# Memory attention's softmax placed ahead of its value tiles, and the first value tile of the recurrence placed ahead of its diagonal products

## The chip, the cores and the metric

The kernel runs on one core of one Trainium2 chip. The metric is the device time of one execution in microseconds (us), as the median of several runs. The profile is one further execution, recorded by the hardware profiler.

## What is computed

The reference is a stack of transformer layers over 256 tokens of width 1024, all in float32: a gated feed-forward layer, a mixer of two attentions, cross attention over 256 memory tokens, a second feed-forward layer, then an RWKV-7 layer (the recurrence), a squared-ReLU layer, sliding-window attention and a last squared-ReLU layer. The change touches the cross attention and the recurrence:

```python
def memory_cross_attention(h, mem_n, w_q, w_kv, w_o):
    b, s, _ = h.shape
    q = (h @ w_q).reshape(b, s, MEM_HEADS, MEM_HEAD_DIM) * (MEM_HEAD_DIM ** -0.5)
    k, v = jnp.split(mem_n @ w_kv, 2, axis=-1)
    k = k.reshape(b, -1, MEM_HEADS, MEM_HEAD_DIM)
    v = v.reshape(b, -1, MEM_HEADS, MEM_HEAD_DIM)
    p = jax.nn.softmax(jnp.einsum('bshd,bmhd->bhsm', q, k).astype(jnp.float32), axis=-1)
    o = jnp.einsum('bhsm,bmhd->bshd', p.astype(v.dtype), v).reshape(b, s, D_MODEL)
    return o @ w_o
```

There are 4 memory heads of width 256. In the recurrence, `r, k, v` are three products with token-shifted inputs, the keys are scaled and normalised per head (`kk / max(sqrt(sum(kk * kk)), 1e-12)`), `g` is a two-step low-rank gate, and per head the state is updated token by token:

```python
    def step(S, inp):
        r_t, w_t, k_t, v_t, a_t, b_t = inp
        sa = jnp.einsum('bhvk,bhk->bhv', S, a_t)
        S = S * w_t[:, :, None, :] + sa[..., None] * b_t[:, :, None, :] + v_t[..., None] * k_t[:, :, None, :]
        y = jnp.einsum('bhvk,bhk->bhv', S, r_t)
        return S, y
```

The kernel computes it by chunks of 128 tokens: 16 heads times 2 chunks give 32 triangular matrices that are inverted, from 32x32 blocks on the diagonal outwards.

## The kernel before

**Weights.** All weights stream through a ring of four slots, one tile of 128x2048 floats (1 MB) each. A large product is done in three passes (`product`, L355 to L357): the weights are split into a high part (copy on ScalarE, L305, `heads_after`) and a low part (subtraction on VectorE, L315, `rests_after`), half a tile at a time, into four half slots. `heads_after(done)` and `rests_after(done)` issue every split whose slot was freed by a half tile of index below `done`; since engines run their instructions in order, a call that waits for TensorE to end a tile stops everything behind it on that engine. `multiplied(g)` waits for tile g's products (`tile_done`, which counts two per tile). The value tiles of the recurrence and the tile `lora_g` are used whole (`arrived_raw`), without a split; each of their products takes all of float32's passes.

**Memory stage** (`memory_stage`, L1745). TensorE: four key tiles, four query tiles, the scores of two token halves t (L1814) in banks 0 to 3, four value tiles in banks 4 to 7 (`col_to_natural`), with the transposes of the weights of half 0 (`turn(0)`, L1788) after the third value tile and of half 1 after the fourth, then the value products (L1828), t by t, head by head, once every value tile is copied, then the output tiles (`out_stage("memo")`), which wait for the split of the values: three of four parts ahead of the first tile. VectorE: `largest(t)` scales the scores and takes the maximum (L1877, L1880), `weigh(t)` divides by the sum (L1884, L1886). ScalarE: exponentials with sums (L1851), copies of the value tiles (L1857), of the turned weights (L1862) and of the values (L1867). On ScalarE the exponentials of half t stand in round n = 8 + t, behind `heads_before` of that round, which waits for the first value tile in round 8. Softmax and value tiles are interleaved in the same rounds.

**Recurrence, projections** (`rwkv_projections`, L1991). After the last key tile, TensorE sums the squares of the keys (L2230), does the tail of the gate's first product (L2217), waits for the inverse norms, spreads them over the channels (L2238) and does the rest of the gate's first product (`lora_g_in`, L2223). ScalarE takes the root of the sums (L2350) and two sigmoids (L2352, L2353). VectorE makes `undirected` (L2147), `decayed` (L2150) and one column (L2172), then the inverse norms (L2175 and the reciprocal L2176), two parts of keys and reads, and multiplies by the spread norms (L2181, L2182). The stage is a block of its own: all engines meet at its end.

**Recurrence, inverses** (`rwkv_inverses`, L2379). TensorE: diagonal 32x32 products (L2453) and 128x128 grams (L2444) in two rounds, two more grams, the gate's second product (L2465, L2469), then the value tiles as fillers: `values()` is a generator that issues one of its 64 products (L2481) per step, and `fill(n)` issues n of them between the groups of small products; `fill(16)` ahead of the bonus (L2493) and the transposes `turn(0)`, `turn(1)`, further ones after the step products (L2524), the 32-row products (L2534), the narrow (L2542, L2544) and cross products (L2553 to L2555), and four in each round of the last loop (L2563, L2568). VectorE solves the diagonal blocks in a long chain (`solve_blocks`, L2730) and turns the result by L2632 (`t16`), for which L2524 waits. Its small copies follow each group. POOL clears buffers.

Engines synchronise by semaphores (`wait_ge`, `then_inc`); `at(k)` counts from the stage's start, `since(k)` from a mark.

Of the kernel before, what the change touches and what calls it, by code (L numbers as in the profile page):

```python
# [25 lines left out]
P = 128  # L26
SEQ = 256
TT = SEQ // P
D = 1024
KC = D // P  # L30
# [8 lines left out]
MEM_HEADS = 4  # L39
# [1081 lines left out]
def mixer_section(e):  # L1121
    nc = e.nc
    with ExitStack() as stack:
# [40 lines left out]
        out_stage(e, "memo", om, [("ffn2_norm", e.hT)], ready=e.sig("memory_split"), needs=(3, 3, 4, 4))  # L1164
# [579 lines left out]

def memory_stage(e, memory, om):  # L1745
# [18 lines left out]
    with Open(nc) as block, ExitStack() as stack:  # L1764
# [9 lines left out]
        def _(pe):  # L1774
# [42 lines left out]
            for n in range(4):  # L1817
                col_to_natural(e, pe, g_v + n, memory.T, 4 + n)
                if n == 2:
                    turn(0)  # L1820
            turn(1)
            for t in range(TT):
                pe.wait_ge(*turned_copied.at(t + 1))
                pe.wait_ge(*evacuated[0].at(8))
                for h in range(MEM_HEADS):
                    for c in range(2):
                        for kb in range(TT):
                            mm = pe.matmul(e.ps[:, 2 * t + h // 2, span(2 * (h % 2) + c, P)],  # L1828
                                           memory.vm[:, kb, span(2 * h + c, P)], pT[t][:, h, kb, :],
                                           start=(kb == 0), stop=(kb == TT - 1))  # L1830
                    if h % 2:
                        mm.then_inc(*values_ready.one())

        @block.scalar
        def _(act):
# [4 lines left out]
            for n in range(12):  # L1840
                heads_before(e, act, g_k + n + 1)
# [5 lines left out]
                if n in (8, 9):  # L1847
                    t = n - 8
                    act.wait_ge(*max_ready.at(t + 1))
                    for h in range(MEM_HEADS):  # L1850
                        x = act.activation(scores[t][:, h, :], scores[t][:, h, :], ACT.Exp, bias=stat[:, t, 0, h:h + 1],  # L1851
                                           accum_out=stat[:, t, 1, h:h + 1])
                    x.then_inc(*sums_ready.one())
                if n >= 8:
                    multiplied(e, act, g_k + n)
                    for t in range(TT):
# [3 lines left out]
            for t in range(TT):  # L1860
                act.wait_ge(*turned.at(t + 1))
                act.activation(pT[t].rearrange("p h k n -> p (h k n)"),  # L1862
                               e.ps[:, 2 * t:2 * t + 2, :].rearrange("p b n -> p (b n)"), ACT.Copy).then_inc(*turned_copied.one())
            heads_after(e, act, 2 * (g_k + 12))
            for b in range(4):
                act.wait_ge(*values_ready.at(b + 1))
# [4 lines left out]
        def _(dve):  # L1871
# [22 lines left out]
            for n in range(12):  # L1894
                if n == 8:
                    largest(0)
                rests_before(e, dve, g_k + n + 1)
# [17 lines left out]
            for b in range(4):  # L1915
                dve.wait_ge(*headed.at(b + 1))
                at = (ALL, span(b % 2, 4), span(b // 2, P))
                dve.tensor_tensor(om[1][at], e.ps[:, b, :].rearrange("p (c n) -> p c n", c=4), om[0][at].bitcast(F32),
                                  ALU.subtract).then_inc(*split.one())
# [70 lines left out]

def rwkv_projections(e, w):  # L1991
# [13 lines left out]
    gained, before_ready = e.sig("hidden_ready"), e.sig("hidden_hi_ready")  # L2005
# [28 lines left out]
    with nc.Block() as block:  # L2034
# [13 lines left out]
        def _(dve):  # L2048
# [115 lines left out]
            undirected(2)  # L2164
            multiplied(e, dve, first[K] + 3)
# [8 lines left out]
            dve.wait_ge(*root.at(2))  # L2174
            link.done(dve.tensor_scalar(inv[:, 0, :], inv[:, 0, :], 1e-12, None, ALU.max))  # L2175
# [1422 lines left out]
```

## Time and profile before

| | us |
|---|---|
| median of 3 runs | 1420.87 (1419.27 to 1429.3) |
| time of the profiled execution | 1425.83 |
| its span, first to last instruction | 1424.5 |
| TensorE busy (matmul) | 1369.2 (96%) |
| VectorE busy | 913.7 (64%) |
| ScalarE busy | 706.0 (50%) |
| mean granted TensorE clock | 0.983 |
| median time of a 1 MB tile from issue to landing | 4.8 |

PE is TensorE, PEld its weight loads, DVE VectorE, ACT ScalarE, POOL GpSimd, SP the engine that issues the loads. The granted clock is a share of 2.4 GHz: 1.00 or, at the lower of its two levels, 0.50 (1.2 GHz); values between are means over both. Matmuls overlap, so that one product lasts longer than the distance to the next. Times in the views count from the first instruction.

### The profile page before, as it was taken

The page shows a single profiled execution, that of the slowest core. Times are in us where ns is not written, and L with a number is a line of the kernel's source. Part 1 is how long each engine was busy: PE and PEld are TensorE (multiplying, and loading weights), DVE is VectorE, ACT ScalarE, POOL GpSimd, SP SyncE. Part 2 cuts the span into 40 slices and gives each one's busy share as a digit, 9 for nine tenths or more (in the row PEclk, how much of TensorE's full clock was granted, in tenths as well). Part 3 has the DMA queues.
Part 4 walks back from the last instruction along what each step waited for, and adds up shares of the span by engine and source line. Part 5 has one row for each costly group of instructions (what it writes and reads, how often), then busy time and mean ns, then how long its engine had stood idle before and what let it go on. Part 6 is the DMA issues. An engine that isn't in the chain of part 4 may idle for free. (4 is left out here: it accounts for less than half of the span.)

```text
span 1424.5 us, 28869 instructions
## 1 busy us (share of the span) xinstructions
PE 1369.2 (96%) x12692; PEld 1309.6 (92%) x12692; DVE 913.7 (64%) x1419; ACT 706.0 (50%) x1098; POOL 8.2 (1%) x14
## 2 busy tenths in 40 slices
PE   8999999999899999999999799999999997999999
PEld 8999999888899899999998587889999995899999
DVE  4766566467775447666689863567666677576665
ACT  5544455266464446444457323345454466454443
POOL 0000000000000000000000010000000000000000
PEclk9999999999999999999999999999999999999999
DMA  7555555451344334555524021104645542245542
GB/s 271 207 193 197 202 180 201 183 231 38 144 182 166 130 119 149 208 203 181 198 103 178 31 91 60 61 22 163 231 178 188 206 154 75 90 170 205 187 178 89
DMA packets 33109, 222.48 MB, mean 156 GB/s; under 512 B 3879, under 2 KB 5295, under 8 KB 6616
## 3 DMA queue, kind: packets, MB, share of 16 engines
q1 hardware_dynamic: 31928, 219.57, 42.6%
q8 instruction: 100, 1.64, 0.5%
q10 hardware_dynamic: 1056, 1.07, 0.2%
q14 instruction: 25, 0.20, 0.0%
HBM read 219.55 MB, written 1.07 MB: 155 GB/s over the span
## 5 line engine op out<-in xcount | busy, mean ns | idle before, releaser
L315 DVE TENSOR_TENSOR tile_lo<-ring,tile_hi 128x1024 fp32r<-128x1024 f32 x388 | 465.9, 1222 | 277.4 <-ACT tile_hi L305 276.7
L305 ACT ACTIVATE tile_hi<-ring 128x1024 fp32r<-128x1024 f32 x388 | 400.0, 1054 | 254.7 <-PE ps L357 248.9
L355 PE MATMUL ps<-hT_hi,tile_hi 128*128 128x256 f32 x1664 | 464.9, 279 | 5.0 <-DVE tile_lo L315 1.8
L356 PE MATMUL ps<-hT_lo,tile_hi 128*128 128x256 f32 x1664 | 460.8, 277 | 0.0
L357 PE MATMUL ps<-hT_hi,tile_lo 128*128 128x256 f32 x1664 | 460.7, 277 | 0.0
L355 PEld LDWEIGHTS ps<-hT_hi,tile_hi 128*128 128x128 f32 x1664 | 312.8, 188 | 10.6 <-issue 4.7
L356 PEld LDWEIGHTS ps<-hT_lo,tile_hi 128*128 128x128 f32 x1664 | 312.8, 188 | 0.0
L357 PEld LDWEIGHTS ps<-hT_hi,tile_lo 128*128 128x128 f32 x1664 | 312.6, 188 | 0.0
L355 PE MATMUL ps<-hidden_hi,tile_hi 128*128 128x256 f32 x864 | 239.7, 277 | 0.0
L356 PE MATMUL ps<-hidden_lo,tile_hi 128*128 128x256 f32 x864 | 239.7, 277 | 0.0
L357 PE MATMUL ps<-hidden_hi,tile_lo 128*128 128x256 f32 x864 | 239.7, 277 | 0.0
L357 PEld LDWEIGHTS ps<-hidden_hi,tile_lo 128*128 128x128 f32 x864 | 162.3, 188 | 0.0
L355 PEld LDWEIGHTS ps<-hidden_hi,tile_hi 128*128 128x128 f32 x864 | 162.3, 188 | 0.0
L356 PEld LDWEIGHTS ps<-hidden_lo,tile_hi 128*128 128x128 f32 x864 | 162.2, 188 | 0.0
L736 ACT ACTIVATE hidden_hi<-hidden_whole 128x512 fp32r<-128x512 f32 x54 | 34.1, 632 | 113.5 <-DVE hidden_whole L774 65.2
L789 DVE TENSOR_TENSOR hidden_lo<-hidden_whole,hidden_hi 128x512 fp32r<-128x512 f32 x54 | 37.4, 692 | 39.2 <-ACT hidden_hi L736 33.1
L780 DVE TENSOR_TENSOR hidden_whole<-gate,token_scale 128x512 f32<-128x512 f32 x32 | 22.1, 692 | 31.1 <-ACT gate L731 31.1
L1064 ACT ACTIVATE scores<-scores,lane_stats 128x128 f32<-128x128 f32 (+3 forms) x80 | 35.4, 445 | 8.8 <-DVE lane_stats L1090 8.8
L731 ACT ACTIVATE gate<-ps 128x512 f32<-128x512 f32 x32 | 19.0, 595 | 41.4 <-PE ps L357 41.4
L355 PE MATMUL ps<-y_turned,tile_hi 128*128 128x256 f32 x128 | 36.0, 281 | 2.1 <-DVE tile_lo L315 2.1
L726 ACT ACTIVATE gate<-gate 128x512 f32<-128x512 f32 x22 | 13.9, 632 | 45.2 <-DVE gate L768 45.2
L357 PE MATMUL ps<-y_turned,tile_lo 128*128 128x256 f32 x128 | 35.6, 278 | 0.0
(465 smaller groups left out, 2012.3 us busy)
## 6 DMA issues: line engine op xcount, KB each, us to landing
ring<-stream SPq DMA_DIRECT2D x204, 1024.0 KB, 4.8
x_sb<-x SPq DMA_DIRECT2D x4, 256.0 KB, 3.8
bias<-f_dram ACTq DMA_DIRECT2D x1, 1024.0 KB, 8.1
fox_bias<-forget_dram SPq DMA_DIRECT2D x1, 1024.0 KB, 7.5
squares<-mem SPq DMA_DIRECT2D x1, 1024.0 KB, 4.7
out<-x_sb SPq DMA_DIRECT2D x4, 256.0 KB, 2.2
const_sb<-const SPq DMA_DIRECT2D x1, 581.0 KB, 9.4
small_sb<-small SPq DMA_DIRECT2D x1, 493.5 KB, 9.8
```

The source lines that it names most:

```text
L305: act.activation(e.w_hi[:, n % SPLIT, :], e.ring[:, tile % RING, span(n % 2, HALF)], ACT.Copy).then_inc(e.tile_hi.handle, 1)
L315: dve.tensor_tensor(e.w_lo[:, n % SPLIT, :], e.ring[:, CUT[n // 2] % RING, span(n % 2, HALF)], e.w_hi[:, n % SPLIT, :].bitcast(F32), ALU.s ...
L355: pe.matmul(out, left[0], right[0], start=start, stop=False)
L356: pe.matmul(out, left[0], right[1], start=False, stop=False)
L357: return pe.matmul(out, left[1], right[0], start=False, stop=stop)
L726: act.activation(tmp[:, j % 2, :], tmp[:, j % 2, :], ACT.Silu).then_inc(*act_done.one())
L731: act.activation(tmp[:, j % 2, :], e.ps[:, up_bank(j, 0), :], ACT.Relu).then_inc(*act_done.one())
L736: act.activation(slot(0, j), whole[:, j % 2, :], ACT.Copy).then_inc(*hi_ready.one())
L780: link.done(dve.tensor_tensor(halves_of(both), halves_of(tmp[:, j % 2, :]), scale_pairs(e), ALU.mult))
L789: dve.tensor_tensor(slot(1, j), both, slot(0, j).bitcast(F32), ALU.subtract).then_inc(*hidden_ready.one())
L1064: x = act.activation(summed(step)[:, lane], summed(step)[:, lane], ACT.Exp, bias=st[:, 0, lane:lane + 1], accum_out=st[:, 1, lane:lane + 1])
```

## The change

In the memory stage the softmax is placed ahead of the splits of the later value tiles, the transposes come after the second and third value tile, the value products go by heads (0 and 1, then 2, then 3) with both token halves inside, and the first output tiles wait for two of four parts. In the recurrence the inverse norms are made ahead of the decayed keys, the first value tile is multiplied at the end of the projections, into bank 3, and the fillers in the inverses shrink by its 16 products. The signal of the gate tile counts four instead of two, for the gate tile and the first value tile together.

```diff
-        out_stage(e, "memo", om, [("ffn2_norm", e.hT)], ready=e.sig("memory_split"), needs=(3, 3, 4, 4))
+        out_stage(e, "memo", om, [("ffn2_norm", e.hT)], ready=e.sig("memory_split"), needs=(2, 2, 4, 4))
...
+VALUE_BANKS = (0, 2, 1, 3)
...
             for n in range(4):
                 col_to_natural(e, pe, g_v + n, memory.T, 4 + n)
-                if n == 2:
-                    turn(0)
-            turn(1)
-            for t in range(TT):
-                pe.wait_ge(*turned_copied.at(t + 1))
-                pe.wait_ge(*evacuated[0].at(8))
-                for h in range(MEM_HEADS):
-                    for c in range(2):
-                        for kb in range(TT):
-                            mm = pe.matmul(e.ps[:, 2 * t + h // 2, span(2 * (h % 2) + c, P)],
...
+                if n in (1, 2):
+                    turn(n - 1)
+            pe.wait_ge(*turned_copied.at(2))
+            for heads in ((0, 1), (2,), (3,)):
+                pe.wait_ge(*evacuated[0].at(5 + heads[-1]))
+                for t in range(TT):
+                    for h in heads:
+                        for c in range(2):
+                            for kb in range(TT):
+                                mm = pe.matmul(e.ps[:, 2 * t + h // 2, span(2 * (h % 2) + c, P)],
...
             for n in range(12):
+                if n == 8:
+                    heads_after(e, act, 2 * g_v)
+                    for t in range(TT):
+                        act.wait_ge(*max_ready.at(t + 1))
+                        for h in range(MEM_HEADS):
+                            x = act.activation(scores[t][:, h, :], scores[t][:, h, :], ACT.Exp, bias=stat[:, t, 0, h:h + 1],
+                                               accum_out=stat[:, t, 1, h:h + 1])
+                        x.then_inc(*sums_ready.one())
                 heads_before(e, act, g_k + n + 1)
...
-                if n in (8, 9):
-                    t = n - 8
-                    act.wait_ge(*max_ready.at(t + 1))
...
                 if n >= 8:
                     multiplied(e, act, g_k + n)
+                    if n < 11:
+                        heads_after(e, act, 2 * (g_k + n) + 2)
...
-            for t in range(TT):
-                act.wait_ge(*turned.at(t + 1))
-                act.activation(pT[t].rearrange("p h k n -> p (h k n)"),
...
+                if n in (9, 10):
+                    t = n - 9
+                    act.wait_ge(*turned.at(t + 1))
+                    act.activation(pT[t].rearrange("p h k n -> p (h k n)"),
...
             for n in range(12):
                 if n == 8:
                     largest(0)
+                    rests_after(e, dve, 2 * g_v)
+                    largest(1)
+                    weigh(0)
+                    weigh(1)
                 rests_before(e, dve, g_k + n + 1)
...
-                if n == 8:
-                    largest(1)
-                if n in (9, 10):
-                    weigh(n - 9)
...
+VALUE_BANK = 3
...
             dve.wait_ge(*evacuated.at(7))
             undirected(2)
+            dve.wait_ge(*root.at(2))
+            link.done(dve.tensor_scalar(inv[:, 0, :], inv[:, 0, :], 1e-12, None, ALU.max))
+            dve.reciprocal(inv[:, 1, :], inv[:, 0, :]).then_inc(*inv_ready.one())
             multiplied(e, dve, first[K] + 3)
...
-            dve.wait_ge(*root.at(2))
-            link.done(dve.tensor_scalar(inv[:, 0, :], inv[:, 0, :], 1e-12, None, ALU.max))
-            dve.reciprocal(inv[:, 1, :], inv[:, 0, :]).then_inc(*inv_ready.one())
             keys_of_k(2)
...
+            def first_values():
+                weights = arrived_raw(e, pe, FIRST["v"]).rearrange("p (m k n) -> p m k n", m=2, k=KC)
+                for t in range(TT):
+                    for k in range(KC):
+                        mm = pe.matmul(e.ps[:, VALUE_BANK, span(t, 256)].rearrange("p (m n) -> p m n", m=2),
+                                       xs[V][:, k, span(t, P)], weights[:, :, k, :], start=k == 0, stop=k == KC - 1)
+                mm.then_inc(*first_valued.one())
...
             lora_g_in()
+            pe.wait_ge(*evacuated.at(8))
+            first_values()
...
                 mm.then_inc(*diag_done.one())
+                if g == 1:
+                    pe.wait_ge(*values_copied.at(1))
                 gram(g)
...
-                mm.then_inc(*e.tile_done.one(2))
+                mm.then_inc(*e.tile_done.one(4))
...
-                for i, bank in enumerate(value_banks):
+                for i, bank in list(enumerate(value_banks))[1:]:
...
-            fill(16)
+            fill(8)
...
-                fill((3, 5)[g])
+                fill(3)
...
-                fill((3, 5)[g])
+                fill(3)
...
-                fill((3, 4)[g])
+                fill(3)
...
-                fill(3)
+                fill(2)
```

On ScalarE the copy of the first value tile comes first in the inverses, ahead of the copies of the grams; it came after the gate's copies. The copies of the memory values and their subtractions follow `VALUE_BANKS`.

## Rows read from the trace of the kernel before

**Rows 1.** the profile page, busy time of each engine; costliest groups, one row
```profile
PE 1369.2 (96%) x12692; PEld 1309.6 (92%) x12692; DVE 913.7 (64%) x1419; ACT 706.0 (50%) x1098; POOL 8.2 (1%) x14
...
L315 DVE TENSOR_TENSOR tile_lo<-ring,tile_hi 128x1024 fp32r<-128x1024 f32 x388 | 465.9, 1222 | 277.4 <-ACT tile_hi L305 276.7
```

**Rows 2.** TensorE's waits: line waited for, us in total, times, longest
```profile
PE ps L2238 <- DVE cum L2176: 5.5, 1, 5.5
```

**Rows 3.** timeline of TensorE, memory stage: start, us, engine, line, names, count, [idle before]
```profile
489.95 0.38 PE L355 MATMUL ps<-tile_hi,memT_hi 128*128 128x256 f32 x1 [1.87 <-DVE tile_lo L315]
...
497.24 1.03 PE L1788 MATMUL ps<-const_sb,bias 128*128 128x128 f32 x8
...
506.78 9.04 PE L1828 MATMUL ps<-queries,mem_kv 128*128 128x128 f32 x64 [1.97 <-ACT queries L1862]
515.58 0.36 PE L355 MATMUL ps<-y_turned,tile_hi 128*128 128x256 f32 x1
```

**Rows 4.** timeline of ScalarE, memory stage
```profile
482.52 1.06 ACT L305 ACTIVATE tile_hi<-ring 128x1024 fp32r<-128x1024 f32 x1 [12.10 <-PE ps L357]
483.59 1.28 ACT L1851 ACT_TABLE_LOAD   x1
...
486.87 0.81 ACT L1857 ACTIVATE mem_kv<-ps,norm_stats 128x256 f32<-128x256 f32 x2
...
504.99 0.82 ACT L1857 ACTIVATE mem_kv<-ps,norm_stats 128x256 f32<-128x256 f32 x2
```

**Rows 5.** timeline of VectorE, memory stage
```profile
474.79 1.22 DVE L1880 TENSOR_REDUCE memory_stats<-bias 128x4 f32<-128x1024 f32 x1
...
484.75 1.40 DVE L1877 TENSOR_SCALAR bias<-ps,norm_stats 128x512 f32<-128x512 f32 x2
...
491.15 1.14 DVE L1886 TENSOR_SCALAR bias<-bias,memory_stats 128x256 f32<-128x256 f32 x4
```

**Rows 6.** windows of 2 us, memory stage: busy PE PEld DVE ACT POOL, PEclk, DMA, GB/s
```profile
492.00:494.00 2.00, 2.00 (x11) 2.00 (x11) 1.04 (x3) 1.21 (x2) 0.00 (x0) 0.50 0.92 385
```

**Rows 7.** timeline of TensorE, recurrence
```profile
799.09 2.09 PE L2238 MATMUL ps<-cum,const_sb 32*128 32x256 f32 x16 [5.53 <-DVE cum L2176]
801.11 5.60 PE L2223 MATMUL ps<-v_rwkv,ring 128*128 128x256 f32 x16
807.72 1.28 PE L2453 MATMUL ps<-AR,spare 64*32 64x32 f32 x128 [1.00 <-PEq L2034]
...
820.48 7.07 PE L2481 MATMUL ps<-ring,mixed_values 128*128 128x256 f32 x32
...
831.88 1.77 PE L2524 MATMUL ps<-cum,diagonal_upper 32*32 32x32 f32 x128
...
839.66 1.29 PE L2534 MATMUL ps<-diagonal_plain,before 32*32 32x32 f32 x128
```

**Rows 8.** timeline of VectorE, recurrence
```profile
793.89 1.87 DVE L2150 SCALAR_TENSOR_TENSOR AR<-spare,ep 128x508 f32<-128x508 f32 x3
...
797.29 1.75 DVE L2176 RECIPROCAL cum<-cum 128x256 f32<-128x256 f32 x1
...
827.30 1.96 DVE L2632 STREAM_TRANSPOSE cum<-cum 128x1024 f32<-128x1024 f32 x1
...
842.05 0.71 DVE L2651 STREAM_TRANSPOSE diagonal_upper<-diagonal_plain 128x512 f32<-128x512 f32 x1
```

**Rows 9.** timeline of ScalarE, recurrence
```profile
791.03 0.38 ACT L2350 ACTIVATE cum<-ps 128x256 f32<-128x256 f32 x1
...
807.03 0.38 ACT L2353 ACTIVATE gate_hidden<-ps 128x256 f32<-128x256 f32 x1
```

**Rows 10.** windows in the recurrence, same columns as rows 6
```profile
802.00:804.00 2.00, 2.00 (x6) 1.55 (x6) 2.00 (x4) 0.00 (x0) 0.00 (x0) 0.50 0.00 0
...
832.00:834.00 2.00, 2.00 (x129) 1.94 (x126) 1.47 (x2) 0.89 (x3) 0.65 (x1) 0.57 0.03 8
...
888.00:889.00 1.00, 1.00 (x6) 0.83 (x8) 0.00 (x0) 0.00 (x0) 0.00 (x0) 0.50 0.00 0
```

More of the change, by code:

```diff
@@ L1859, in _ @@
                     x.then_inc(*evacuated[0].one())
-            for t in range(TT):
-                act.wait_ge(*turned.at(t + 1))
-                act.activation(pT[t].rearrange("p h k n -> p (h k n)"),
-                               e.ps[:, 2 * t:2 * t + 2, :].rearrange("p b n -> p (b n)"), ACT.Copy).then_inc(*turned_copied.one())
+                if n in (9, 10):
+                    t = n - 9
+                    act.wait_ge(*turned.at(t + 1))
+                    act.activation(pT[t].rearrange("p h k n -> p (h k n)"),
+                                   e.ps[:, 2 * t:2 * t + 2, :].rearrange("p b n -> p (b n)"),
+                                   ACT.Copy).then_inc(*turned_copied.one())
             heads_after(e, act, 2 * (g_k + 12))
-            for b in range(4):
-                act.wait_ge(*values_ready.at(b + 1))
+            for at, b in enumerate(VALUE_BANKS):
+                act.wait_ge(*values_ready.at(at + 1))
                 act.activation(om[0][:, span(b % 2, 4), span(b // 2, P)], e.ps[:, b, :].rearrange("p (c n) -> p c n", c=4),
@@ L1909, in _ @@
                                       ALU.mult).then_inc(*query_scale.one())
-                if n == 8:
-                    largest(1)
-                if n in (9, 10):
-                    weigh(n - 9)
             rests_after(e, dve, 2 * (g_k + 12))
[L1915 to L1918, printed above, removed]
+            for at, b in enumerate(VALUE_BANKS):
+                dve.wait_ge(*headed.at(at + 1))
+                part = (ALL, span(b % 2, 4), span(b // 2, P))
+                dve.tensor_tensor(om[1][part], e.ps[:, b, :].rearrange("p (c n) -> p c n", c=4), om[0][part].bitcast(F32),
                                   ALU.subtract).then_inc(*split.one())
@@ L2669, in _, with value_copy @@
             copy = lambda dst, src: act.activation(dst, src, ACT.Copy)
+            def value_copy(i):
+                if i == 0:
+                    act.wait_ge(*first_valued.since(1))
+                else:
+                    multiplied(e, act, g_v + i)
+                copy(w.v[:, :, i * 256:(i + 1) * 256],
+                     e.ps[:, value_banks[i], :].rearrange("p (t n) -> p t n", t=TT)).then_inc(*values_copied.one())
+            value_copy(0)
             for i in range(4):
@@ L2678, in turned_copy @@
                 copy((v.b_nat, v.k_nat)[n // 2][:, span(n % 2, 512)], e.ps[:, 6 + n % 2, :]).then_inc(*copied.one())
-            def value_copy(i):
-                multiplied(e, act, g_v + i)
-                copy(w.v[:, :, i * 256:(i + 1) * 256],
-                     e.ps[:, value_banks[i], :].rearrange("p (t n) -> p t n", t=TT)).then_inc(*values_copied.one())
             for b in range(4):
```

17 lines of the change are left out of this document (6 added, 11 removed).

## The prediction

> **What bounds the kernel now.** The busy line of the page comes first: TensorE is busy for 1369.2 of 1424.5 us [rows 1]. So an edit on another engine pays only where TensorE stands still or runs at its lower clock, and moving TensorE work pays only if it lands in such a place. The list of TensorE's waits gives 5.5 us ahead of L2238 (the spread of the inverse norms, waiting for the reciprocal at L2176) [rows 2]. The timeline of TensorE in the memory stage adds two that the diff touches: 1.87 us ahead of the third value tile, which waits for its low half, and 1.97 us ahead of L1828 (memory values, waiting for the copy of the turned weights at L1862) [rows 3]. The windows show what each pause costs besides: after it the granted clock stands at 0.50 (1.2 instead of 2.4 GHz) [rows 6, 10].
>
> **Memory stage, waits removed.** Before, ScalarE takes the high half of value tile 3 only when tile 1 is done (482.52), then loads the exponential's table (1.28 us) and does four exponentials (done by 486.87, where the copy of the first value tile starts) [rows 4]. The maxima of the first token half are ready at 476.0 (474.79 + 1.22), but the second half's scores are read only at 484.75 [rows 5]. All of this stands ahead of the second half of value tile 3. The change puts it into the 12 us in which ScalarE idled before 482.52. In the new order: table load and exponentials of half 0 from 476.1 to 479.4 (1.28 + 2.0); on VectorE one tile subtraction (1.2, the group's mean) [rows 1] and the maxima of half 1 (1.40 + 1.22, the two rows from 484.75 and 474.79) from 476.0 to 479.9; exponentials of half 1 to 481.9; the weighing of each half 1.3 us (1.14 at 491.15 and the reciprocal), the last to 483.3. Value tile 1 ends at 482.4, so both high halves of tile 3 are there at 484.6, both low ones at 486.0. Tile 2 ends at 488.08 (489.95 less 1.87) [rows 3]. The 1.87 us go, with 2.1 us to spare.
>
> TensorE then does turn(0), tile 3, turn(1), tile 4, the values. Both turns now lie a whole tile (5.6 us) ahead of the values, and the copy of turned weights takes 1 us (505.8, where the copy of tile 4 ends, to 506.78) [rows 3, 4], so the 1.97 us ahead of L1828 go too [rows 3]. What is late next: the copy of tile 4. Before, it ended at 505.8 (504.99 + 0.82) [rows 4], about 2 us after its tile. With heads 0, 1 and 2 put first, three quarters of the value products (some 5 us) cover it. The output stage now needs both halves of heads 0 and 1 split: copies and subtractions of 0.6 and 0.7 us after half the value products, done some 2 us before TensorE ends the rest. So (2, 2, 4, 4) costs nothing. That the tile splits of the output weights come a little later is covered by the same value products.
>
> **Memory stage, the clock.** Tile 3 took from 489.95 to 497.24, 7.29 us, against 5.6 for tile 2 (482.45 to 488.08): 1.7 for the lower clock. The values took 8.8 us (506.78 to 515.58); by the pitch of the eight 128x128 products at L1788, (1.03 - 0.27)/7 = 0.108 us, the 64 take 6.95: 1.8 [rows 3, 6]. With the pauses gone both go. Sum: 1.87 + 1.97 + 1.7 + 1.8 = 7.3; I take 7.2. Bounds: 3.8 if the low stretches are only displaced, 7.4 at most.
>
> **Recurrence, inverse norms.** The root is ready at 791.4 [rows 9], but the reciprocal ends at 799.04 (797.29 + 1.75), behind the decayed keys that begin at 793.9 [rows 8]. In the new order the maximum (0.3) and the reciprocal (1.75) start at 793.9 and end at 796.0. So the spread starts 3.05 us earlier, at 796.0. VectorE's own work stays in one piece and ends no later than before.
>
> **Recurrence, first value tile.** Spread and gate products took 7.62 us (799.09 to 806.71) [rows 7], at the lower clock for much of it [rows 10]. At these durations they end at 803.6; the value tile follows, 7.07 us (L2481 at 820.48), to 810.7. The block before ended with ScalarE's two sigmoids at 807.4 [rows 9] and the diagonal products began 0.3 later, at 807.72; now they begin at 811.0, which is 3.3 us later. Bounds of this delay: 1.2, if the clock is up again when the spread is done (gate products 3.5 instead of 5.6); 10.3, if all the value tile runs at 1.2 GHz (7.07 more). I take 3.3, the durations of the rows. Its weights are loaded once the second key tile is split, over 20 us earlier, where a load takes some 5 us, and the copy of the tile, 0.6 us on an idle ScalarE, is done before gram(1) needs bank 3: nothing. The earlier release of the ring slot (one(4)) only lets one load start sooner: nothing.
>
> **Recurrence, inside the inverse stage.** From the diagonal products to the step products TensorE took 24.16 us without a real pause (807.72 to 831.88). Eight of 16 value products less are 3.54 (7.07/2) [rows 7]. But the step products also need the turned inverses of VectorE, ready at 827.30 + 1.96 = 829.26, 21.54 after the diagonal products [rows 8]. So the gain is 24.16 - 21.6 = 2.5, and TensorE waits 1 us for VectorE. After that fills shrink by seven and the last round by one more: eight at 0.44, 3.5 us, if TensorE stays the bound there. It should: a group of 128 small products takes 1.3 us (839.66) and three fills 1.3, while VectorE's copies and transpose are done 1.8 us after such a group ends (842.76 against 840.95) [rows 7, 8], and nobody needs them until another group and two runs of fills later, 3.9 us. Sum of the recurrence: -2.5 - 3.5 + 3.3 = -2.7.
>
> **The sum.** -7.2 - 2.7 = -9.9 against the profiled execution: 1425.83 - 9.9 = 1415.9 (its span is 1424.5; the 1.3 us around it stay). That execution is 5 us above the median of the runs, 1420.87 (1419.27 to 1429.3), with the same program; what differs must lie in stretches like those at the lower clock. For the median I therefore count only half of the memory stage's clock terms (1.8 less), and half of one such stretch (0.8) as won in the recurrence, where the pause shrinks from 5.5 to 2.5 us: gain 8.9, time 1412.0.
>
> The Trainium skill ("TensorE: Matmul & The Clock Gate", section on what is actually happening in the clock gate) says that where the clock changes differs from run to run of one kernel. The spread of the three times agrees; by this rule the clock terms are an average, which is how they were halved. A second page, "ScalarE: Activation LUTs", section "What ACT_TABLE_LOAD costs", adds about 1.4 us of draining to each table load; the row shows 1.28 and the first exponential right behind it. By the page the spare time of tile 3 would be about 1 us and not 2.
>
> **Rivals.**
> A, the softmax is late all the same. Two engines pass the work to each other four times before tile 3 can be split, and the spare time is 2.1 us. If it runs out, a pause with its low stretch returns: up to 1.9 + 1.7, so 1415.6. Against it: ScalarE and VectorE have nothing else to do in this time. Chance 0.12.
> B, the fills were hidden. If VectorE's copies bind the groups after the step products, the last 3.5 us are not won, the recurrence comes out at +0.8, and the time is 1415.5. For it: it binds already at the step products. Chance 0.15.
> C, more is won elsewhere. The tail of the recurrence stands at 0.50 clock around 888 [rows 10], in the rounds of its loop. If the changed entry spares it two or three low stretches of 1.7 each, the time is about 1407. Chance 0.15.
> D, slower than before: the thinned-out fills let the clock fall in the inverse stage. The fills are the only large products among groups of 32x32 ones; around 833, after the bonus products, the clock was 0.57 for once [rows 10]. Every further stretch at 1.2 GHz costs 1.7. The change loses from six of them on (9.9/1.7), of the 13 that fit into the 44 us after the step products; with eight, 1412.0 + 13.6 = 1425.6. Against it: TensorE stays busy between them but for 1 us. Chance 0.04.
> The rest, 0.54, is the forecast, 1408 to 1416 by itself.
>
> **How the numbers follow.** A measurement of this kernel tells about 1% from no change, 14.2 us. Faster by more needs 1406.7 or less: half of C and an edge of the forecast, 0.14. Slower by more needs 1435.1: part of D, 0.02. Within 1%: 0.84. The range takes in A and B, C's nearer half and the slow edge where the low stretches only move: 1404.5 to 1419.5.
>
> **What would show it.** Right: no wait ahead of the third value tile and of L1828, output products starting about 7 us earlier after the scores than before; the wait ahead of L2238 near 2.5 us; diagonal products 3 us later after the last key product; about 1 us of waiting for VectorE's transposes at the step products; from the diagonal products to the tail's first product 68.5 - 6 us. Wrong: a wait for a low half in the value tiles, waits at the copies after the step products, or a clock of 0.5 over the value tile or the small groups.

## The result and the profile after

The changed kernel takes 1412.75 us (median of 20 runs, 1407.93 to 1429.17); the kernel before took 1421.87 us beside it (20 runs). The ratio is 0.9927, with a 95% interval of 0.9909 to 0.9946. The ratios leave disturbed runs out, so that they differ a little from the quotient of the medians. The forecast of 1412.0 us stands within 1 us of it, and the change is inside 1%, as forecast. The sum behind the forecast was less right than its total, and that is what the experiments are about.

TensorE is busy for about as long as before (1372.8 us against 1369.2 [rows 1]). Its busy line on the page, and its waits (line, total, times, longest):

```profile
PE 1372.8 (97%) x12692; PEld 1314.1 (92%) x12692; DVE 913.7 (64%) x1419; ACT 706.0 (50%) x1098; POOL 8.2 (1%) x14
...
PE ps L355 <- DVE tile_lo L315: 7.0, 8, 1.5
PE ps L2249 <- DVE cum L2178: 2.6, 1, 2.6
...
PE ps L2504 <- issue: 2.2, 1, 2.2
```

The wait for the reciprocal fell from 5.5 [rows 2] to 2.6 us, and nothing waits at L1831 (L1828 before). The last line, time in which TensorE waits for nothing that the profile shows ("issue"), is not new but longer; before it was one gap of 0.94 us:

```profile
846.48 1.24 PE L2481 MATMUL ps<-ring,mixed_values 128*128 128x256 f32 x5 [0.94 <-issue]
```

**Memory stage.** The timeline of TensorE after (start, us, engine, line, names, count, idle before in brackets):

```profile
473.39 7.14 PE L1817 MATMUL ps<-mem_kv,fox_bias 128*128 128x256 f32 x32 [0.78 <-ACT fox_bias L1855]
...
491.68 1.04 PE L1791 MATMUL ps<-const_sb,bias 128*128 128x128 f32 x8
492.47 0.36 PE L355 MATMUL ps<-tile_hi,memT_hi 128*128 128x256 f32 x1
...
498.21 1.03 PE L1791 MATMUL ps<-const_sb,bias 128*128 128x128 f32 x8
...
504.74 7.30 PE L1831 MATMUL ps<-queries,mem_kv 128*128 128x128 f32 x64
```

Neither the third value tile (it begins at 492.47) nor the value products have a bracket, and the 64 value products last 7.30 us instead of 9.04 [rows 3]. The timeline of ScalarE there:

```profile
474.21 1.28 ACT L1849 ACT_TABLE_LOAD   x1
479.82 0.51 ACT L1849 ACTIVATE bias<-bias,memory_stats 128x256 f32<-128x256 f32 x1 [4.33 <-DVE memory_stats L1888]
...
486.28 2.01 ACT L305 ACTIVATE tile_hi<-ring 128x1024 fp32r<-128x1024 f32 x2 [0.68 <-PE ps L357]
```

The exponentials lie in ScalarE's old pause, and both high halves of the third value tile are taken at 486.28, 12.9 us after the scores begin (before, the second of them was taken at 487.58, 18.0 after):

```profile
487.58 1.99 ACT L305 ACTIVATE tile_hi<-ring 128x1024 fp32r<-128x1024 f32 x2
```

The windows (columns as in rows 6) stand at full clock where rows 6 had 0.50:

```profile
490.00:492.00 2.00, 2.00 (x19) 2.00 (x18) 0.00 (x0) 0.06 (x1) 0.00 (x0) 1.00 0.63 143
498.00:500.00 2.00, 2.00 (x20) 2.00 (x19) 0.44 (x1) 1.53 (x2) 0.00 (x0) 1.00 0.77 324
```

**Recurrence.** TensorE's timeline after, from the spread of the inverse norms to the second 32-row group:

```profile
792.55 2.09 PE L2249 MATMUL ps<-cum,const_sb 32*128 32x256 f32 x16 [2.56 <-DVE cum L2178]
794.57 5.90 PE L2234 MATMUL ps<-v_rwkv,ring 128*128 128x256 f32 x16
800.31 7.07 PE L2258 MATMUL ps<-ring,mixed_values 128*128 128x256 f32 x32
807.70 1.28 PE L2474 MATMUL ps<-AR,spare 64*32 64x32 f32 x128 [0.33 <-PEq L2045]
...
829.37 1.77 PE L2547 MATMUL ps<-cum,diagonal_upper 32*32 32x32 f32 x128
831.07 2.57 PE L2504 MATMUL ps<-ring,mixed_values 128*128 128x256 f32 x6
833.57 1.29 PE L2547 MATMUL ps<-cum,diagonal_upper 32*32 32x32 f32 x128
...
836.61 1.28 PE L2557 MATMUL ps<-diagonal_plain,before 32*32 32x32 f32 x128 [0.26 <-issue]
840.07 2.72 PE L2504 MATMUL ps<-ring,mixed_values 128*128 128x256 f32 x6 [2.18 <-issue]
```

VectorE there: the reciprocal, the last key of the block, and the turned inverses that the step products wait for (rows 8 before):

```profile
790.75 1.75 DVE L2178 RECIPROCAL cum<-cum 128x256 f32<-128x256 f32 x1
...
800.95 0.68 DVE L2193 TENSOR_TENSOR AR<-AR,ps 128x512 f32<-128x512 f32 x1
...
827.34 1.97 DVE L2655 STREAM_TRANSPOSE cum<-cum 128x1024 f32<-128x1024 f32 x1
```

In one table, the stretches between fixed instructions of TensorE in the profiled execution of each kernel (us; "memory": start of the first score product to start of the last value product; "block end": first norm sum to first diagonal product; "solve": from there to the first step product; "groups": from there to the first product of the tail):

| kernel | memory | block end | solve | groups | issue gaps in "groups" | ratio to before (95%) |
|---|---|---|---|---|---|---|
| before | 45.9 | 17.8 | 24.2 | 44.3 | 0.40, 0.94 | |
| after | 38.4 | 21.4 | 21.7 | 43.1 | 0.26, 2.18 | 0.9927 (0.9909 to 0.9946) |
| changed_again | 38.4 | 18.2 | 22.2 | 42.1 | 2.46, 1.05 | 0.9933 (0.9900 to 0.9967) |
| mem_only | 38.4 | 17.0 | 25.3 | 43.9 | 0.72, 0.73 | 0.9950 (0.9937 to 0.9964) |
| rec_only | 44.4 | 19.9 | 21.6 | 44.7 | 0.41, 2.72 | 0.9996 (0.9981 to 1.0011) |
| gate_first_no_value | 45.9 | 15.6 | 26.1 | 44.4 | 0.25, 1.22 | 0.9999 (0.9983 to 1.0016) |
| gate_first | 38.4 | 15.8 | 21.7 | 43.6 | 0.29, 2.46, 0.26 | 0.9939 (0.9922 to 0.9955) |
| fills_early | 38.4 | 19.7 | 21.8 | 40.2 | 0.56, 1.00 | 0.9924 (0.9891 to 0.9957) |
| gate_first_fills_early | 38.4 | 15.8 | 21.5 | 40.6 | 1.36, 1.00, 0.24 | 0.9909 (0.9876 to 0.9941) |
| the same, second time | 38.4 | 15.8 | 22.0 | 41.0 | 0.56, 1.00, 0.16 | 0.9863 (0.9847 to 0.9880) |
| late_turns | 39.8 | 19.9 | 22.0 | 43.1 | 2.73, 1.32, 0.34 | 0.9973 (0.9938 to 1.0009) |
| late_softmax | 41.0 | 19.8 | 21.7 | 43.1 | 0.60, 2.46, 1.32 | 0.9969 (0.9936 to 1.0001) |
| late_norms | 38.4 | 23.7 | 22.0 | 44.0 | 0.34, 2.46 | 0.9915 (0.9896 to 0.9934) |
| norms_only | 45.9 | 15.6 | 25.5 | 45.0 | 0.63, 1.22 | 1.0027 (0.9984 to 1.0070) |

A stage repeats within a few tenths of a microsecond where its clock does, and by some 3 us where the clock differs (block end: 21.4, 18.2, 19.7, 19.9 for the same program there, in after, changed_again, fills_early and late_turns). The rest of the program differs by several us between executions: the scores begin at 469.6 before and 473.4 after, though nothing ahead of them was changed. So stages are compared by the table, totals by the ratios. Each row of the table is one execution.

### The profile page after: what moved, and what is told of

It reads as the page before. It is cut to its first block and busy times, and to the rows that moved or that the text cites. A ratio compares the mean times of both kernels' runs of the same rounds, so it can differ in the third digit from the quotient of the medians.

```text
span 1422.4 us, 28871 instructions
## 1 busy us (share of the span) xinstructions
PE 1372.8 (97%) x12692; PEld 1314.1 (92%) x12692; DVE 913.7 (64%) x1419; ACT 706.0 (50%) x1098; POOL 8.2 (1%) x14
## 5 line engine op out<-in xcount | busy, mean ns | idle before, releaser
L355 PE MATMUL ps<-y_turned,tile_hi 128*128 128x256 f32 x128 | 35.8, 280 | 2.9 <-DVE tile_lo L315 2.9
L356 PE MATMUL ps<-y_turned,tile_hi 128*128 128x256 f32 x128 | 35.4, 277 | 0.0
```

The source lines that it names most:

```text
L355: pe.matmul(out, left[0], right[0], start=start, stop=False)
L356: pe.matmul(out, left[0], right[1], start=False, stop=False)
```

## The experiments

**Each half alone.** mem_only has the change of the memory stage (the hunks from `out_stage` to the value copies), rec_only all the others.

> Only the memory stage's part of the change, the recurrence as before. Theory S (the sum of the prediction): the pauses ahead of the third value tile and of the value products are gone, scores to first output product 7.2 us shorter than the 45.96 of before in a trace that has no low clock there, 5.4 us less on average, so about 1416.5. Rival Z (the recurrence's part gives nothing, the memory stage gives all): 9 us less, about 1413.

> Only the recurrence's part, the memory stage as before. Theory S: 2.7 to 3.5 us less, about 1418.5; last key product to diagonal products some 3.3 us longer (18.9 to 22.3), diagonal to step products 2.5 shorter (24.2 to 21.7), step products to the first product of the tail 3.5 shorter (44.3 to 40.8). Rival Z: the last of these is only 1 us shorter, because the gaps that TensorE shows as issue and the low clock there come with the thinned fills, and the time is that of before, 1421.9.

Measured: mem_only 1412.3 us (6 runs) and rec_only 1419.39 us (12 runs) beside 1420.52 us before. The memory half gives 0.5% (7.1 us by the ratio, 5.1 to 8.9 by its interval) and has its 7.5 us in the stage; the time is nearer to rival Z's 1413 than to theory S's 1416.5. The recurrence half gives nothing that its interval can tell from none: +2.1 at the block's end, -2.6 in the solve, +0.4 in the groups. There theory S missed (40.8 us forecast for the groups, 44.7 measured) and rival Z holds. Its timeline of TensorE has the new gap again, at the same place:

```profile
838.69 1.29 PE L2549 MATMUL ps<-diagonal_plain,before 32*32 32x32 f32 x128 [0.41 <-issue]
...
842.70 2.93 PE L2496 MATMUL ps<-ring,mixed_values 128*128 128x256 f32 x6 [2.72 <-issue]
```

**The pause ahead of the spread.** The gate products need nothing of the inverse norms, so they can stand in the pause:

```diff
-            norm_spread()
             pe.wait_ge(*evacuated.at(7))
             lora_g_in()
+            norm_spread()
```

gate_first is the changed kernel with this edit. gate_first_no_value has it on the kernel before, with the early inverse norms but with neither the first value tile nor the smaller fills.

> The changed kernel with the rest of the gate's first product put ahead of the spread of the inverse norms, so that it fills the 2.6 us in which TensorE waits for the reciprocal. Theory W (the pause and the low clock that follows it are real cost on the path): gate products at full clock take 3.5 us, spread from then on, value tile done about 5 us sooner, last key product to diagonal products 17.5 instead of 22.5, time about 1408. Rival V (VectorE's products with the spread norms end the block): they end at least 16 us after the last key product, so less than 2 us can be won, and with the spread 1 us later nothing: 1412.

> Before, with the inverse norms early and the gate products ahead of the spread, the first value tile left among the fills of the inverse stage and the memory stage as before. Theory W: the block now ends with VectorE, about 16.3 us after the last key product, so the diagonal products start 2 to 2.5 us sooner than before: about 1419. If this kernel were as fast against before as gate_first is against the changed kernel (4 to 5 us), the value tile's move itself would be worth nothing; theory W wants it to be worth some 6 us once the pause is filled, since it then stands beside VectorE's work.

Measured: gate_first 1409.43 us (6 runs), gate_first_no_value 1419.93 us (12 runs), before 1420.52. The timeline of TensorE in gate_first:

```profile
785.68 3.72 PE L2234 MATMUL ps<-v_rwkv,ring 128*128 128x256 f32 x16
789.34 1.15 PE L2249 MATMUL ps<-cum,const_sb 32*128 32x256 f32 x16
790.41 7.17 PE L2258 MATMUL ps<-ring,mixed_values 128*128 128x256 f32 x32
```

No bracket is left, and the gate products last 3.72 us and not 5.90. In gate_first_no_value, without the value tile, the block ends hardly sooner:

```profile
795.23 1.15 PE L2238 MATMUL ps<-cum,const_sb 32*128 32x256 f32 x16
...
803.56 1.54 PE L2453 MATMUL ps<-AR,spare 64*32 64x32 f32 x128 [7.19 <-PEq L2034]
```

TensorE waits 7.2 us at the end of the block for VectorE's last keys. So with this edit VectorE ends the block, and of the 7.2 us of the first value tile all but 0.2 lie in that wait: 15.8 against 15.6 us. In the stage theory W holds: the block of gate_first ends 2.4 to 5.6 us sooner than in the two executions of the changed kernel. In the total it doesn't show: 0.9939 is no better than the changed kernel's 0.9927, and 1412 us (by the ratio) is what rival V had. Nor do the totals show the 6 us that theory W wanted of the value tile's move. The stages of the recurrence give 5.0 us from gate_first_no_value to gate_first (+0.2, -4.4, -0.8); in the ratios gate_first is 8.5 us better, of which the memory half is 7.1.

**The changed kernel again, and the fills.** changed_again is the changed kernel unaltered, to see its spread. fills_early takes eight filler products from the last loop and puts two more behind each group of step products and of 32-row products; gate_first_fills_early has this and the gate products ahead of the spread:

```diff
                 mm.then_inc(*step_done.one())
-                fill(3)
+                fill(5)
...
                 mm.then_inc(*a32_done.one())
-                fill(3)
+                fill(5)
```

> The changed kernel itself, once more, as the yardstick for the runs beside it: about 1412.5, with the same stage lengths as its first trace but for the clock, and again one gap of 2 to 2.7 us called issue in the value products after the second group of 32x32 products.

> The changed kernel with five instead of three fills after each of the first four groups of small products, and so eight fewer in the last loop. Theory F (the groups of 256 instructions in 1.3 us outrun TensorE's instruction loads, and fills between them are free as long as they stand in such a gap): the gap called issue falls from 2.2 to 2.7 us to about 1.3 or less, as before the change; step products to the first product of the tail 1 to 2.5 us shorter than 43.4, about 1411. Rival G (the gap has nothing to do with the fills): it stays, the groups take 3.5 us longer, the last loop gives 2 to 3.5 back: same time or up to 1.5 us slower.

> Both versions together: the gate products ahead of the spread and the fills early. Theories W and F: 4 to 5 us and 1 to 2.5 us less than the changed kernel, 1406 to 1408. By the rivals V and G 1412.

> The version of two edits once more (gate products ahead of the spread, the value products of the fills put earlier, into the rounds of the step products), for a narrower interval. If the edits add up: 0.991 of the kernel before, 2 to 5 us below the changed kernel's 1412. If the earlier value was luck: 0.9925, as the changed kernel itself.

Measured: changed_again 1410.32 us, fills_early 1410.97, gate_first_fills_early 1407.17 (6 runs each) beside 1420.16 before; the second time 1412.83 (4 runs) beside 1430.11, in a batch in which the kernel before was slower. The timeline of TensorE in changed_again shows both findings of this study at once:

```profile
787.97 1.15 PE L2249 MATMUL ps<-cum,const_sb 32*128 32x256 f32 x16 [2.55 <-DVE cum L2178]
789.05 3.72 PE L2234 MATMUL ps<-v_rwkv,ring 128*128 128x256 f32 x16
...
832.08 1.46 PE L2504 MATMUL ps<-ring,mixed_values 128*128 128x256 f32 x6 [2.46 <-issue]
835.73 0.26 PE L2557 MATMUL ps<-diagonal_plain,before 32*32 32x32 f32 x7 [1.05 <-issue]
```

The same pause of 2.55 us was not followed by the lower clock this time (5.90 against 3.72 us for the same products), which is the 3 us between 21.4 and 18.2. And the gaps at the groups come back in the same program. In fills_early they are smaller:

```profile
834.12 1.78 PE L2504 MATMUL ps<-ring,mixed_values 128*128 128x256 f32 x7 [0.56 <-issue]
838.05 0.26 PE L2557 MATMUL ps<-diagonal_plain,before 32*32 32x32 f32 x8 [1.00 <-issue]
```

The stretch of the groups is 40.2 us, with the same products in it, against 43.1 and 42.1: the eight products cost less there than they did in the last loop. In the ratios fills_early alone can't be told from the changed kernel, so the total is also what rival G had. Both edits together are 0.9909 and 0.9863 of the kernel before. Beside the changed kernel they were run once, and are 3 us below it (1407.17 and 1410.32) with intervals that overlap. The second time the changed kernel was not run beside them, and the kernel before spread from 1420 to 1435 us. The two ratios of one program are 0.0046 apart, so ratios of different batches are not compared more finely than that. That both edits together win in the total is likely and not shown.

**Parts of the memory stage.** late_turns moves only the two transposes of the changed kernel one value tile later (`if n in (2, 3): turn(n - 2)`). late_softmax has this, and the softmax back behind the first value tiles as before the change; the order of the heads and the new order of splits and copies on ScalarE stay.

> The changed kernel with the transposes of the memory weights back behind the third and fourth value tile. Theory S: the copy of the second turned half stands again between the last transposes and the value products: 1.9 to 2.0 us of waiting ahead of them, with the low clock up to 3.8 us more than the changed kernel; scores to last value product 40.3 to 42.1 instead of 38.4. Rival: the value products of heads 0 and 1 need only one half at first, so nothing is lost; it falls if the wait is there, since TensorE waits for both halves.

> The changed kernel with the memory attention's softmax back behind the first value tiles (exponentials in rounds 8 and 9, maxima and weighing one tile later, turns behind tiles 3 and 4); the order of the heads and everything in the recurrence stay as changed. Theory S (the late softmax is what the 7.5 us of this stage come from): TensorE waits again ahead of the third value tile, about 1.9 us, and about 1.1 to 2 us ahead of the memory values; first score product to last value product 43.8 to 45.9 us where the changed kernel has 38.4; the whole 5 to 7 us above the changed kernel, so near 0.997 of the kernel before. Rival H (the order of the heads does part of it): the stage below 42 us.

Measured: late_turns 1418.66 us (4 runs), 39.8 us for the stage, under theory S's range of 40.3 to 42.1; late_softmax 1426.57 us (10 runs, beside 1430.11 before), 41.0 us, so theory S missed its range of 43.8 to 45.9 and H's bound of 42 holds. The waits themselves came back, in late_softmax ahead of the third value tile and of the value products, in late_turns only ahead of the latter. The timelines of TensorE, late_softmax first:

```profile
492.19 0.39 PE L355 MATMUL ps<-tile_hi,memT_hi 128*128 128x256 f32 x1 [1.16 <-DVE tile_lo L315]
...
506.42 7.41 PE L1831 MATMUL ps<-queries,mem_kv 128*128 128x128 f32 x64 [1.11 <-ACT queries L1868]
```

```profile
509.02 7.41 PE L1831 MATMUL ps<-queries,mem_kv 128*128 128x128 f32 x64 [1.11 <-ACT queries L1869]
```

But they are 1.1 us long instead of 1.9 to 2.0, and the windows of late_softmax behind them stay at full clock:

```profile
492.00:494.00 2.00, 1.81 (x16) 1.81 (x17) 1.53 (x4) 2.00 (x8) 0.00 (x0) 1.00 0.34 66
...
506.00:508.00 2.00, 1.58 (x14) 1.58 (x15) 0.66 (x1) 2.00 (x5) 0.00 (x0) 1.00 0.92 365
```

So of the stage's 7.5 us, the place of the softmax and of the transposes is worth 2.6 (2.3 of pauses), and 4.9 came with what late_softmax kept: pauses shorter by 0.7 and 0.9 us, and 3.3 us that the clock would have taken. Which of the kept edits (the heads' order, or that ScalarE now splits the next tile before it copies this one) shortened each pause was not run apart. The totals don't divide the same way: 0.9973 and 0.9969 are 6 us above the changed kernel's 0.9927, as theory S had it for late_softmax ("near 0.997"), though their intervals overlap with its own. The profile of late_softmax is the second fastest of its ten executions (1417.84 us), so its 41.0 us are a good case, and the division of the 7.5 us holds for the profiled executions.

Nor does a pause of 1.9 us always cost its clock. rec_only has the memory stage of before, and after its first pause the clock stays at 1.00 (timeline of TensorE, and the window behind the pause):

```profile
490.92 0.39 PE L355 MATMUL ps<-tile_hi,memT_hi 128*128 128x256 f32 x1 [1.88 <-DVE tile_lo L315]
...
492.00:494.00 2.00, 2.00 (x20) 2.00 (x19) 1.23 (x5) 2.00 (x6) 0.00 (x0) 1.00 0.73 283
```

This is the 1.5 us between its 44.4 and the 45.9 of before.

**Inverse norms.** late_norms puts them back behind the decayed keys in the changed kernel; norms_only is the kernel before with them early.

> The changed kernel with the inverse norms back behind the decayed keys; the first value tile stays ahead of the diagonal products. Theory N (the early inverse norms matter in the changed kernel, since TensorE's own work now ends the block): a wait of about 5.5 us ahead of the spread, first norm sum to first diagonal product 3 us longer than the 21.4 of the changed kernel, about 24.4, and the whole 2 to 3 us above it. Rival K (the granted clock gives it back): the block within 1.5 us of 21.4.

> The kernel before with one part of the change alone: the inverse norms ahead of the decayed keys. Theory V (in the block before, VectorE's last key tile ends it once TensorE's wait is cut): the wait ahead of the spread is 2.5 us, first norm sum to first diagonal product 15.6 to 16.5 us where the kernel before has 17.8, with a wait of TensorE ahead of the diagonal products; ratio 0.997 to 1.000. Rival W (TensorE's chain ends the block in full): 14.8 us, three less than before.

Measured: late_norms 1419.77 us (4 runs), norms_only 1435.53 us (10 runs), beside 1430.11. The timelines of TensorE, late_norms and then norms_only:

```profile
791.93 2.09 PE L2249 MATMUL ps<-cum,const_sb 32*128 32x256 f32 x16 [5.62 <-DVE cum L2187]
```

```profile
812.55 1.28 PE L2453 MATMUL ps<-AR,spare 64*32 64x32 f32 x128 [2.88 <-PEq L2034]
```

Theory N holds in the stage (wait 5.62 us, block end 23.7 us, 2.3 above the longest of the changed kernel's), but not in the total: 0.9915 is not above the changed kernel's 0.9927, and the interval of each is some 2.7 us to either side, as much as was looked for. V holds in the stage too: in the kernel before, the early norms end the block 2.3 us sooner (15.6 against 17.8), and then VectorE is the last. The total shows none of it (0.9984 to 1.0070).

## Why the prediction was right, and which steps were not

| step of the prediction | forecast | measured |
|---|---|---|
| memory stage, both pauses and their clock | -7.2 (3.8 to 7.4) | -7.5 |
| wait ahead of the spread | near 2.5 | 2.56 (2.55 in changed_again) |
| block end later by | 3.3 (1.2 to 10.3) | 3.6; 0.4 in changed_again |
| diagonal to step products | -2.5 | -2.5; -2.0 in changed_again |
| rest of the fills | -3.5 | -1.2; -2.2 in changed_again; +0.4 in rec_only |
| sum of the four stages | -9.9 | -7.6; -11.3 in changed_again |

**Right, mechanism and size.** The memory stage lost both pauses and both low stretches (7.5 us, just above the bound of 7.4), and no wait took their place; rival A is out. The third value tile's low half is there at 489.73 (487.37 + 2.36 on VectorE), 1.95 us before TensorE is done with tile 2 at 491.68, where the prediction had 2.1 to spare; the shorter time of about 1 us, which it worked out beside this, did not come true. The inverse norms halved the wait. The solve ends with VectorE now as forecast: the step products begin at 829.37, when the transpose ends (827.34 + 1.97 = 829.31), and in all ten kernels with the moved value tile they begin 0.05 to 0.54 us after it, where before it was 2.62. The 1 us of waiting for it was not seen as such. TensorE had lost about half of it earlier, in gaps called "issue" among the diagonal products (1.16 and 0.27 us after the change, 0.96 before), and most of the rest in the grams that follow them. What binds is as said, what fills the slack is not.

**The step that failed inside the sum** is "After that fills shrink by seven and the last round by one more: eight at 0.44, 3.5 us, if TensorE stays the bound there". It won 1.2 us in the changed kernel (2.2 in changed_again) and nothing in rec_only. Rival B had the size (nothing of the 3.5) but not the cause: it looked for VectorE's copies, and no wait for a copy stands there. The engine waits for nothing that the profile shows. In the windows of the changed kernel (columns as in rows 6):

```profile
838.00:840.00 2.00, 0.00 (x0) 0.00 (x1) 1.56 (x3) 0.74 (x2) 0.00 (x0) 0.99 0.00 0
840.00:842.00 2.00, 1.93 (x5) 1.55 (x5) 0.00 (x0) 0.00 (x0) 0.00 (x0) 0.50 0.03 8
```

For 2 us TensorE does nothing, while the filler product that comes next has its weights and its inputs (other products of the same tile ran before the gap), and the clock after that is 0.50: a part of the gain is paid as gap, a part as clock.

Where the loss lies shows when the stretch is cut at the first narrow product (the first after the four groups; starts of TensorE's products, us):

| kernels | fills within the four groups | first step product to first narrow product | from there to the tail |
|---|---|---|---|
| before, mem_only, gate_first_no_value, norms_only | 16 | 15.3 to 16.4 (before 15.8) | 28.55 |
| after, changed_again, rec_only, gate_first, late_turns, late_softmax, late_norms | 12 | 15.3 to 17.9 (after 16.3) | 26.8 (26.82 or 26.83) |
| fills_early, gate_first_fills_early (twice) | 20 | 17.1 to 17.6 | 23.1 to 23.4 |

So the four fills taken out behind the groups gave 1.7 us in every kernel, as forecast (4 times 0.44), and the four taken out between the groups gave nothing.

The size fits the supply of instructions. The list of queues of the changed kernel has one queue of instruction loads with 100 of them, and a window from 836 to 840 us has one load and no other transfer:

```profile
q8 instruction: 100, 1.64, 0.4%
...
q8 instruction: 1, 0.02, 1.5%
```

The page counts 12692 matmuls and as many weight loads on TensorE, 25384 instructions, or 254 for each of the 100 loads. A group of 128 small products has 256 such instructions and takes 1.3 us. But the loads come no faster than one in 3.3 us in the traces of before, after and changed_again; between 830 and 842 us of the changed kernel they start at 830.4, 834.5, 837.8 and 841.3. And each gap ends with a load. That of 2.18 us ends at 840.07, and the load that began at 837.76 had landed at 838.70, 1.37 us earlier. In the 14 profiles there are 56 gaps called "issue" on TensorE from 760 to 900 us, and every one of them ends 1.2 to 1.6 us (mean 1.39) after a load has landed; with one load in about 3.6 us, chance would put one gap in nine there. In before, after and changed_again TensorE has no such gap anywhere else in the program. From the start of the load the distance varies about twice as much (2.15 to 2.71 us), so the end of the gap goes with the landing.

So the fills that were taken away between the groups stood in time that the instructions took anyway, and came back as gap and low clock. Thinning the fills opens the gap at the same place (2.18 to 2.73 us in after, rec_only, gate_first, changed_again, late_norms, late_softmax and late_turns, 0.73 to 1.22 at most where the fills are whole), and fills put back there shrink it (to 0.56 to 1.36) and shorten the stretch by 1.9 to 3.0 us. That the gaps end with instruction loads is shown by the traces; no run here varied the number of instructions alone, and what holds the loads to one in 3.3 us stays open. The Trainium skill ("Runtime: NRT & Kernel Launch", section "Instruction fetch mechanics") says that instructions are fetched in blocks of 16 KiB, 256 instructions, and that the cost of going from one block to the next is mostly hidden. The size of the load and the count per load agree with the rows; that the cost is hidden doesn't hold in these rounds.

**The block end** was right in its direction and too large on average. Six executions have this program there (after, changed_again, fills_early, late_turns, late_softmax, rec_only): 21.4, 18.2, 19.7, 19.9, 19.8 and 19.9 us, so 2.0 us over the 17.8 of before in the mean, where 3.3 was forecast. Whether the lower clock follows the pause of 2.55 us is open from run to run: windows of the changed kernel's profile stand at 0.50 there,

```profile
796.00:798.00 2.00, 2.00 (x6) 1.63 (x5) 1.97 (x5) 0.00 (x0) 0.00 (x0) 0.50 0.00 0
```

and changed_again's from 787 to 797 at 1.00 throughout. The prediction took the durations of one execution for the term and named 1.2 as the lower bound. The 0.4 of changed_again lies below it, because the spread ran at full clock too (1.15 us instead of 2.09).

**Why the total was so near.** The profiled execution took 1423.67 us, 7.8 above the 1415.9 forecast for it, since 3.8 us were lost ahead of the scores and 3.2 behind the tail, in code that is as before, 2.3 were missing in the four stages, and the tail itself was 1.6 shorter. By the medians the gain is 9.1, forecast 8.9. The memory half measured alone gives 7.1 to 8.2 (by ratio and by medians), more than the 5.4 (7.2 less 1.8) that the forecast counted for it, though 5.4 is still inside its interval; the recurrence half measured alone gives 0.6 to 1.1 of the 3.5 (2.7 and 0.8 for the clock) that it counted, which is outside its interval. These are errors of opposite sign, so that the total came within 1 us is in part luck. From the diagonal products to the tail's first product it was 64.8 us, not the 62.5 forecast. Rival C, the tail: it took from 69.4 to 75.6 us in these profiles, 69.4 in changed_again and 74.0 in after, the same program, so it moved, but not by the change in any way that can be shown. Rival D is out as a price, but a part of it is there: the clock fell once more behind the gap, for a stretch or two and not six, in four of the seven kernels with thinned fills (after, rec_only, gate_first, late_norms). The prediction had named a clock of 0.50 over the small groups as a sign that it is wrong; this sign came, at 840 us.

## What to carry to other kernels

- Filler products between dense groups of tiny ones are not only work that has to go somewhere: they can be the time in which the next instructions come. Before moving them elsewhere, count the instructions per microsecond that are left and look for loads of instructions in the trace. Here a group had 256 instructions in 1.3 us, the loads came one in 3.3 us or more, and two fills fewer behind every second group of 128 took back a third of the gain (after) to all of it (rec_only).
- Work moved from one stage into another is free only where the other stage ends on a different engine. At the block's end the first value tile cost 0.2 us once VectorE ended the block, and 0.4 to 3.6 us with TensorE's pause left in front of it; so first fill the pause with what needs nothing of it (here one call moved), then move work behind it.
- A pause can cost its clock too, and not in every execution. In the profiled ones of the memory stage, pauses of 1.9 to 2.0 us were followed by the low clock in seven of eight cases and those of 1.1 us in none of three, so shortening them from 1.9 to 1.1 won more (4.9 us) than removing the last 1.1 (2.6).

## What was not expected of the hardware

- "Issue" gaps of 2.2 to 2.7 us on TensorE between groups of 32x32 products, in the middle of a stage whose data is all there, each ended by an instruction load that landed 1.2 to 1.6 us before.
- The pauses of 1.11 and 1.16 us in the memory stage left the granted clock at 1.00, those of 1.87 and 1.97 us [rows 3] were followed by 0.50 [rows 6], but one of 1.88 us in rec_only was not; the pause of 2.55 us in the recurrence was followed by 0.50 in after (2.56) and by 1.00 in changed_again.
- The table load of the exponential went ahead of the wait for the maximum (474.21, then 4.33 us of idle time, then the exponential at 479.82); the forecast had it behind the wait. It cost the forecast nothing, since there the exponentials of the second half waited for their maximum (479.9) and not for those of the first (479.4).
